# Every second pair of probability maps combined on GpSimd

## The reference, cut to what matters

```python
def diff_attend(q, k, v, lam):
    s = jnp.einsum('bhiqd,bhikd->bhiqk', q, k).astype(jnp.float32) * (HEAD_DIM ** -0.5)
    p = jax.nn.softmax(s, axis=-1)
    a = (p[:, :, 0] - lam * p[:, :, 1]).astype(v.dtype)
    return jnp.einsum('bhqk,bhkd->bhqd', a, v)
```

## Time and profile before

| | us |
|---|---|
| median of 3 runs | 2620.39 (2618.93 to 2620.96) |
| the profiled execution | 2621.06 |
| its span, first to last instruction | 2619.3 |
| TensorE busy / VectorE / ScalarE / GpSimd | 2505.5 / 1626.1 / 1275.3 / 253.6 |
| `diff_0`, from the first scores | about 1404 to 1490 |
| `diff_1`, from the first scores | about 2270 to 2318 |

### The profile page before, as it was taken

One profiled execution on the slowest core, in us unless ns is written; L12 is line 12 of the kernel. 1 busy time (PEld: TensorE's weight loads), 2 busy tenths in 40 slices (PEclk: granted clock), 3 DMA queues, 4 the chain that ended last, 5 costly groups with the idle time before them and its releaser, 6 DMA issues.

```text
span 2619.3 us, 41629 instructions
## 1 busy us (share of the span) xinstructions
PE 2505.5 (96%) x15930; PEld 2079.9 (79%) x15930; DVE 1626.1 (62%) x2680; ACT 1275.3 (49%) x2372; POOL 253.6 (10%) x266
## 2 busy tenths in 40 slices
PE   6999999999989999999999999899999999999998
PEld 4855678889957999889886687688889899778887
DVE  2657565553688786768776863533326799775664
ACT  3356454433657765533336743422225644675554
POOL 3000100001302100315000001000002330011000
PEclk8999999999999999999999999999999999999999
DMA  7265522224555555534324534522236555634555
GB/s 282 89 227 185 193 96 96 96 88 133 159 178 194 168 180 170 174 109 150 121 97 143 159 122 171 207 96 96 92 94 172 165 178 172 204 107 143 184 173 149
DMA packets 137895, 393.58 MB, mean 150 GB/s; under 512 B 13776, under 2 KB 40400, under 8 KB 137616
## 3 DMA queue, kind: packets, MB, share of 16 engines
q1 hardware_dynamic: 135872, 386.47, 45.5%
q0 software_dynamic: 1872, 5.02, 0.7%
HBM read 390.39 MB, written 1.05 MB: 149 GB/s over the span
## 4 chain that ended last, share of the span: by engine, by line
PE 82%; DVE 8%; ACT 4%; DMA 3%; issue 2%; POOL 1%; SPq 0%; ACTq 0%; DVEq 0%; POOLq 0%
PE bank L647 21%; PE bank L649 20%; PE bank L648 20%; PE bank L644 4%; PE bank L695 3%; PE bank L854 2%; DVE w_low L1863 2%; PE bank L643 2%; PE bank L864 2%; PE bank L879 1%; ACT w_high L1163 1%; DVE smax L2130 1%; PE bank L877 1%; DMA ring<-in_w_down 1%; PE bank L835 1%
## 5 line engine op out<-in xcount | busy, mean ns | idle before, releaser
L1863 DVE TENSOR_TENSOR w_low<-ring,w_high 128x1024 fp32r<-128x1024 f32 (+2 forms) x604 | 688.1, 1141 | 523.8 <-ACT w_high L1163 520.7
L647 PE MATMUL bank<-h_high,w_high 128*128 128x512 f32 (+1 forms) x2576 | 884.2, 343 | 36.2 <-DVE h_low L2060 8.1
L649 PE MATMUL bank<-h_high,w_low 128*128 128x512 f32 (+1 forms) x2576 | 870.5, 338 | 0.0
L648 PE MATMUL bank<-h_low,w_high 128*128 128x256 f32 (+1 forms) x2432 | 821.6, 338 | 0.0
L1163 ACT CAST w_high<-ring 128x1024 fp32r<-128x1024 f32 (+2 forms) x604 | 574.5, 954 | 302.2 <-DMA ring<-in_w_down 146.8
L647 PEld LDWEIGHTS bank<-h_high,w_high 128*128 128x128 f32 x2576 | 493.8, 192 | 98.3 <-issue 24.9
L649 PEld LDWEIGHTS bank<-h_high,w_low 128*128 128x128 f32 x2576 | 493.8, 192 | 50.4
L648 PEld LDWEIGHTS bank<-h_low,w_high 128*128 128x128 f32 x2432 | 465.6, 191 | 49.4 <-issue 1.7
L647 PE MATMUL bank<-f_high,w_high 128*128 128x256 f32 (+1 forms) x616 | 194.7, 316 | 4.1 <-DVE w_low L1863 3.5
L649 PE MATMUL bank<-f_high,w_low 128*128 128x256 f32 (+1 forms) x616 | 193.0, 313 | 0.0
L648 PE MATMUL bank<-f_low,w_high 128*128 128x256 f32 (+1 forms) x528 | 168.1, 318 | 0.0
(11 more groups left out here) (285 smaller groups left out, 3495.4 us busy)
## 6 DMA issues: line engine op xcount, KB each, us to landing
ring<-in_w_up SPq DMA_DIRECT2D x176, 512.0 KB, 3.4
ring<-in_w_mod SPq DMA_DIRECT2D x112, 512.0 KB, 4.2
ring<-in_w_down SPq DMA_DIRECT2D x80, 384.0 KB, 3.1
ring<-in_w_down SPq DMA_DIRECT2D x80, 320.0 KB, 3.0
spare_slabs<-in_w_mod SPq DMA_DIRECT2D x48, 512.0 KB, 8.0
ring<-in_w_gate SPq DMA_DIRECT2D x48, 512.0 KB, 3.4
ring<-in_w_k SPq DMA_DIRECT2D x32, 512.0 KB, 3.5
ring<-in_w_v SPq DMA_DIRECT2D x32, 512.0 KB, 3.4
```

The lines of the kernel that those rows point to most:

```text
L647: pe.matmul(out, wh[:, cols], high, start=first, stop=False)
L648: pe.matmul(out, wh[:, cols], low, start=False, stop=False)
L649: ins = pe.matmul(out, wl[:, cols], high, start=False, stop=last)
L1863: v.tensor_tensor(wl[:, cols], raw[:, cols], wh[:, cols].bitcast(F32), ALU.subtract).then_inc(low_ready, 1)
```

## The change

For every odd unit of `diff_0` and `diff_1`, VectorE stops after the ratio and signals `ratio_ready`. GpSimd, behind its pooling, waits for it, multiplies e1 by the ratio in place, waits for its own result, adds e0, and signals `pr_pool`. TensorE waits for `pr_pool` in odd units and for `pr_ready` in even ones; the counters are adapted. Units of the first block are unchanged.

```diff
--- before.py
+++ after.py
@@ -338,6 +338,7 @@
         hsq_ready, hsum_done, hroot_ready, hnorm_done = sem("head_square"), sem("head_sum"), sem("head_root"), sem("head_norm")
         sc_done, nm_ready, ex_ready, pr_ready = sem("scores_done"), sem("max_ready"), sem("exp_ready"), sem("probs_ready")
         tr_done, pt_ready, pv_done, o_ready = sem("probs_turned"), sem("turned_copied"), sem("pv_done"), sem("o_ready")
+        ratio_ready, pr_pool = sem("map_ratio_ready"), sem("probs_by_pool_ready")
         sig_ready, tap_ready = sem("sigmoid_ready"), sem("conv_centre_ready")
         hid_ready = sem("hidden_ready")
         conv_ready = sem("conv_ready")
@@ -856,7 +857,10 @@
                 def turn(u):
                     for i in range(sets):
                         k = sets * u + i
-                        pe.wait_ge(pr_ready, t0 + k + 1)
+                        if diff:
+                            pe.wait_ge((pr_ready, pr_pool)[u % 2], n["diff" if u % 2 else "probs"] + u // 2 + 1)
+                        else:
+                            pe.wait_ge(pr_ready, n["probs"] + k + 1)
                         if k >= 2:
                             pe.wait_ge(pt_ready, t0 + k - 1)
                         src = PROB[(2 * u + 2 - sets + i) % 6]
@@ -895,6 +899,8 @@
                 n["sub"] += len(units) * 2
                 n["unit"] += len(units)
                 n["turned"] += len(units) * sets
+                n["probs"] += len(units) // 2 if diff else 2 * len(units)
+                n["diff"] += len(units) // 2 if diff else 0
 
             def chunk_ready(count=KC):
                 n["h"] += count
@@ -2150,6 +2156,9 @@
                         v.tensor_scalar(p1, p1, r1, None, ALU.mult).then_inc(pr_ready, 1)
                         return
                     s0 = ssum[:, j % NS:j % NS + 1]
+                    if u % 2:
+                        v.scalar_tensor_tensor(r1, s0, lam, r1, ALU.mult, ALU.mult).then_inc(ratio_ready, 1)
+                        return
                     own.link(v.scalar_tensor_tensor(r1, s0, lam, r1, ALU.mult, ALU.mult))
                     v.scalar_tensor_tensor(p1, p1, r1, p0, ALU.mult, ALU.add).then_inc(pr_ready, 1)
 
@@ -2750,6 +2759,14 @@
                             own.inc(g.tensor_tensor(out[:, s, cols], out[:, s, cols], con[:, at:at + POOL_PAD], ALU.mult))
                     own.wait(own.n)
                     g.tensor_tensor(out, out, PP[:, i, 0:ns, POOL_PAD:POOL_PAD + S], ALU.subtract).then_inc(pool_ready, 1)
+                for u in range(1, len(ATT[f"diff_{l}"]), 2):
+                    n["ratio"] += 1
+                    pool.wait_ge(ratio_ready, n["ratio"])
+                    w = ATT[f"diff_{l}"][u]["T"]
+                    p0, p1 = PROB[2 * u % 6][:, 0:w], PROB[(2 * u + 1) % 6][:, 0:w]
+                    r1 = srec[:, (2 * u + 1) % NS:(2 * u + 1) % NS + 1]
+                    own.link(g.tensor_scalar(p1, p1, r1, None, ALU.mult))
+                    g.tensor_tensor(p1, p1, p0, ALU.add).then_inc(pr_pool, 1)
                 if l == 1:
                     branch, merge = (LIN[f"{k}_1"].empty0["vector"] for k in ("branch", "merge"))
                     for c in range(KC):
```

## The result

The changed kernel takes 2666.40 us (median of 3 runs, 2657.61 to 2668.81) against 2620.39: 1.0169 times as long, 95% interval 1.0132 to 1.0205. Measured again beside other runs it took 2658.85 (2656.78 to 2665.1) against 2620.15, 1.014 times (1.0123 to 1.0157). So it is slower by 39 to 46 us, inside the range of 2641 to 2668, above the 2652 forecast. The profiled execution took 2666.40, with a span of 2664.6 (before: 2619.3).

The account below looks back on a forecast made before the run. TensorE was taken to bound the first attention and to be level with VectorE in the second. Adding 14.3 us (second attention) and 17.2 (first) gave 31.5 on 2620.39: 2652, range 2641 to 2668.

Parts of the forecast that it names:

- What bounds the kernel: TensorE bounds the first attention; in the second TensorE and VectorE are level, 2.54 to 2.57 us a unit.
- Removed: VectorE's combination of every second unit, 0.75 us at 512 columns: counted as zero gain, at most 0.5 us.
- Rival A: Both attentions: the combined map is not late, only VectorE's relief remains, -0.5 us, 2620; chance 3%.
- D: GpSimd's instructions quicker than taken: 2648 or about 2635; anything below 2641 but still slower than before has 5%.
- The way through GpSimd: Odd units, from the ratio's start to TensorE's release: 3.05 us for 512 columns, 2.15 for 256.
- the estimate of 2644: Total time if GpSimd's scaling of 512 columns took 769 ns: 7.7 us less over 16 units.
- Can it hide?: The longer path through GpSimd mostly stays bare: +14.3 us in the second attention, +17.2 in the first.
- Contention: VectorE's two-operand instructions and GpSimd's hold each other up; GpSimd's addition waiting in 16 units of 512 costs +3.5 to +15.5.
- rival B: VectorE slips in between GpSimd's scaling and addition: 2652 plus 3.5 to 15.5, likeliest 2662; chance 17%.
- rival C: TensorE's clock falls in the new gaps: up to +40 us in the second attention, 2692; chance 7%.
- the ring: Second attention: a pair of units becomes one closed chain of waits, 7.05 us instead of 5.14.
- the full range: Total time from 2641 to 2668, the high end being 2652 + 15.5.

Follow-up runs that it names:

- the waits filled: The changed kernel with unread transposes ahead of TensorE's wait for odd maps, twelve in `diff_1`, eight in `diff_0` (units of 512): 2652.34 us, 1.0122 times before.
- the kernel with both orders: The changed kernel with TensorE's previous values ahead of odd transposes and VectorE's odd ratio ahead of the next maxima: 2628.51 us, 1.0027 times before.

## Why the prediction was right, and where it was off

**What bounds the kernel.** Right. In the second attention GpSimd moved into the chain at once, with 33.3%, and in all 8 odd units TensorE waited for it.

**Removed.** Counted at zero, with 0.5 us as the gain's bound. The kernel without those combinations measured 0.9993, with 1.0 inside its interval, and its rings give 0.3 us: right. Rival A (only the relief is left) and D (a quicker GpSimd) fell with it: nothing on GpSimd ran faster than bounded.

**The way through GpSimd.** Predicted 3.05, measured 3.28. The hand-over to GpSimd is 0.32 from the ratio's start (0.22 + 0.15 predicted), the addition 1.26 (1.29), the wait for its own result 0.09 (0.08), the release about 0.05. The one term that was mis-sized is the scaling: 1.562 us on average in 16 units instead of 1.25, inside the bounds of 0.97 and 2.08 and nearer to their middle (1.53) than the value taken. Two instructions of the trace of before that I passed over were nearer: of the four scalings behind the mean of 2.08 in the earlier trace rows those at 1183.61 and 1193.17 took 1.81 and 1.82, and only the two that began beside a running split 2.35. Of one of the latter I had subtracted the whole hold-up; the 1.37 behind it is shorter than 1.56, so if that is its length there too, GpSimd got part of the way during the hold-up. The scaling of the earlier trace rows is by a constant, the new one by a number a row; at 256 columns they take 0.90 and 0.92, so that is hardly the reason. The Trainium skill, GPSIMD Engine Reference, section "Elementwise — side-by-side cycle accounting", has 769 ns for 512 elements; the trace has twice that, and the estimate of 2644 that hung on it does not hold.

**Can it hide?** Right in the second attention: the pair takes 7.32, predicted 7.05. Of the 0.27 between them 0.23 is the way through GpSimd (the scaling 0.31 more, the other terms 0.08 less). At full clock the attention takes 63.3 us, +15.6, predicted 61 to 62, +14.3. In the first attention a head (two odd units) went from 10.18 us (odd ratios of before at 1419.49 and 1429.67) to 12.24 (1421.81 and 1434.05 with the waits filled), +2.06 against 2.04 predicted. This agreement is of two errors: the way was 0.23 too short, and the 0.20 that TensorE comes late at the unit of 256 are taken back at the next unit of 512, whose ratio comes 1.98 us after the scores ahead of it and not 2.17 (1434.05 - 1432.07 against 1429.67 - 1427.50), so that its wait is the shorter. The attention took 102.8 at a clock of 0.98, +16.2, predicted 102 to 103, +17.2. Sum by the medians of before and of the filled waits: +32.2 (2652.34 - 2620.15), predicted +31.5. That the sum agrees so closely is partly luck: the second attention was 1.3 too low and the first 1.0 too high.

**Contention, rival B.** Wrong as a cost. VectorE's ratio and combination of the even unit never came between the scaling and the addition in the second attention: the next ratio starts 2.54 after the odd one, and the addition 1.97. In the first they did once (1410.71 and 1410.97, ahead of the addition at 1411.21), and that addition took 1.36 instead of 1.26. What held the addition once in the second attention was a slab split of VectorE, which the prediction had not named for it:

```profile
2313.82 1.29 DVE L1869 TENSOR_TENSOR w_low<-ring,w_high 128x512 fp32r<-128x512 f32 x2 [0.83 <-ACT w_high L1169]
2314.48 1.76 POOL L2769 TENSOR_TENSOR h_space<-h_space 128x512 f32<-128x512 f32 x1
```

That is 0.50 us longer than the others, in one unit of the 16 of 512. The hold-up falls the other way, as the prediction thought likelier: VectorE's even ratio, 0.22 us long elsewhere, takes 0.70 and ends at 2332.08, where GpSimd's addition ends at 2332.07, and in the first attention a combination of 256 columns, 0.49 us long in before, takes 1.43 beside an addition that ends at 1426.40:

```profile
1425.26 1.43 DVE L2163 SCALAR_TENSOR_TENSOR h_space<-h_space,srec 128x256 f32<-128x256 f32 x1
1425.14 1.26 POOL L2769 TENSOR_TENSOR h_space<-h_space 128x512 f32<-128x512 f32 x1
```

It costs nothing that the rings show, as the even map isn't wanted yet. By the rule of the Trainium skill, SBUF — State Buffer, section "Who interferes with whom", the shared ports are an exclusive lock, and issue order decides who blocks. The trace agrees with it beside the addition, even for an instruction of one column. Beside the scaling, which reads SBUF too, no hold-up shows: the ratio at 1410.71 took its 0.22 while a scaling ran until 1411.13, and the scalings all took 1.56, the one beside the split too. Only the last 0.6 us of a scaling are tried by this.

**The clock, rival C.** This is the step that failed: the sum has nothing for it, and the range was closed without it. I gave it 7%, and only with longer GpSimd instructions than bounded, because the ring keeps 5.14 of 7.05 us of work and the earlier trace rows hold a stretch with 1.90 of 3 at full clock. That compared an average over a ring with one stretch without a long gap. The row that fitted was the other one of the same group: 1.13 of work in 3 us, and a clock of 0.59 behind it. Each ring has such a stretch around its wait of 2.17, and after it the clock fell in some of them (0.53 above) and not in others: from 2330 to 2340 us, with the same waits, it stayed at 1.00. It does not fall for all of the second attention, and so costs, in the profiled executions, 6.2 us in the first attention and 5.5 in the second, 3.7 of them behind the first wait for GpSimd, not the 40 of the rival's bound. In total it is 6.5 us by the medians beside each other; the first median of after, 2666.40, lies 14.1 above that of the filled waits, though not measured beside it. The filled waits show that the gaps are a cause: with them filled the clock is 1.00 from 1412.40 to 1506.70 and in all of the second attention. What decides in which ring it falls is open. Nor is all of the lower clock the change's own: the fall at the start of the second attention comes without any combination on GpSimd as well, and no filling stood there to prevent it.

So the forecast's mechanism held, and its sum, with errors that cancel, for a TensorE that keeps its clock; its own range (2641 to 2658) was too narrow by what the clock costs. That 2666.40 still lies inside the full range is luck: the stretch above 2658 was kept for rival B, which did not happen, and what filled it was the clock, which had been left out, with scatter on top. The second median, 2658.85, lies 0.9 above the forecast's own range.

## What to carry to other kernels

A step that is moved to an idle engine is priced by the way from its input to who waits for it, not by the busy time that it takes off: here an instruction of 0.75 us on VectorE became a way of 3.1 us through GpSimd (3.28 less the ratio's 0.22), bare on the path, for a relief that was worth next to nothing. Before giving work to the slower engine, ask for a place in both queues where its result is wanted late; two changes of order took four fifths of this cost away, but where the relieved engine isn't the bound, what remained here was still a loss. When a clock or a stretch is compared between two profiles, see first whether the difference begins ahead of the edit: here 2.5 us of it did (0.7 ahead of the second attention and 1.8 in it ahead of GpSimd's first instruction). And where a change tears regular gaps of two microseconds into TensorE's work, look for the worst stretch of the new pattern among the clocks of the old trace, not for one with its average share of work.

## What the runs showed of the hardware

- GpSimd's scaling by a number a row is slower than its addition of two maps, though it reads one: 1.562 us against 1.26 at 512 columns, 0.92 against 0.73 at 256, with hardly any scatter (1562 to 1564 ns in 8 units of the kernel with both orders). Doubling the columns costs 0.64 and 0.53.
- Products that do nothing, put into a gap, made a kernel faster by 6.5 us (2658.85 to 2652.34, four executions each); TensorE's granted clock in the second attention went from 0.87 to 1.00, in part by a fall ahead of the gaps that the second execution did not have.
- The clock can fall at the same place of a program in one execution and not in another: from some 2 to 3 us ahead of the second attention's first scores it was down for 6 to 10 us in 7 of 12 profiled executions, with and without work on GpSimd, and at 1.00 there in the other 5. In the changed kernel it was 0.51 from 2295.80 to 2303.90.
- An instruction of one column on VectorE was held 0.48 us by GpSimd's addition (0.70 instead of 0.22), and eight combinations of 256 columns took 1.19 us on average instead of 0.49.
